# Expert loop of a routed MoE layer: index and gate copies moved between ScalarE, GpSimd and VectorE, and bounded gathers

## What is computed

```
scores = sigmoid(xt @ w_router)
_, top_idx = lax.top_k(scores + router_bias, 8)
gates = top_s / sum(top_s) * 2.5
xb = xt[tok_idx]
yb = (silu(xb @ w_gate[e]) * (xb @ w_up[e])) @ w_down[e]
routed = zeros.at[src_tok].add(yb * g[:, None])
```

## Time and profile before

| | us |
|---|---|
| median of 3 runs | 1636.74 |
| lowest, highest | 1635.55, 1638.66 |
| the profiled execution | 1641.21 |
| its span, first to last instruction | 1638.8 |
| busy: PE, DVE, ACT, POOL | 1498.1, 909.0, 562.4, 891.6 |
| mean granted clock of TensorE | 0.974 |

### The profile page before, as it was taken

One profiled execution on the slowest core, in us unless ns is written; L12 is line 12 of the kernel. 1 busy time (PEld: TensorE's weight loads), 2 busy tenths in 40 slices (PEclk: granted clock), 3 DMA queues, 4 the chain that ended last, 5 costly groups with the idle time before them and its releaser, 6 DMA issues.

```text
span 1638.8 us, 28709 instructions
## 1 busy us (share of the span) xinstructions
PE 1498.1 (91%) x9554; PEld 1276.1 (78%) x9554; DVE 909.0 (55%) x1595; ACT 562.4 (34%) x858; POOL 891.6 (54%) x1021
## 2 busy tenths in 40 slices
PE   6999999999799999889999999999999999999980
PEld 5789989989645666778888888888888888888870
DVE  4333788788678764455554454445454454444442
ACT  6434545444433322013333333333333333333333
POOL 0422235063203322467777777777777777777761
PEclk9999999999899999999999999999999999999995
DMA  5389321221250112379999999999999999999966
GB/s 182 98 290 309 120 78 51 77 67 49 103 200 27 41 51 99 121 261 315 327 302 335 308 313 308 315 319 320 315 323 316 316 310 312 325 307 305 321 184 220
DMA packets 104440, 366.18 MB, mean 223 GB/s; under 512 B 25976, under 2 KB 36121, under 8 KB 83407
## 3 DMA queue, kind: packets, MB, share of 16 engines
q1 hardware_dynamic: 60622, 246.60, 40.2%
q0 software_dynamic: 43776, 119.07, 26.8%
HBM read 300.68 MB, written 73.91 MB: 229 GB/s over the span
## 4 chain that ended last, share of the span: by engine, by line
POOL 25%; issue 18%; DMA 10%; POOLq 2%; PE 1%; DVE 1%; ACT 0%; DVEq 0%; ACTq 0%; SPq 0%
POOL wi L1636 16%; DMA acc_rows<-YE,sia 9%; POOL acc_rows L1660 4%; POOL acc_rows L1655 2%; POOL sia L1646 1%; POOL gta L1641 1%; DVE A L1875 1%; PE gu L1713 1%; DMA wi<-xn_rows,gi 1%; POOL sib L1647 0%; POOL gi L1628 0%; POOL gtb L1641 0%; POOLq L1628 0%; DMA A<-acc_rows 0%; POOLq L1687 0%
## 5 line engine op out<-in xcount | busy, mean ns | idle before, releaser
L1713 PE MATMUL gu<-XS,place 128*128 128x160 f32 x4160 | 577.8, 300 | 5.0 <-DVE XS L1829 5.0
L1713 PEld LDWEIGHTS gu<-XS,place 128*128 128x128 f32 x4160 | 573.9, 191 | 10.8 <-DVE XS L1829 5.8
L1636 POOL DMA_INDIRECT wi<-xn_rows,gi x320 | 408.1, 1275 | 132.5 <-issue 77.4
L1829 DVE STREAM_TRANSPOSE XS<-wi 128x1280 f32<-128x1280 f32 x65 | 163.3, 2512 | 369.9 <-DMA wi<-xn_rows,gi 343.4
L1773 ACT ACTIVATE SS<-gu 128x160 f32<-128x160 f32 x130 | 39.5, 304 | 399.0 <-PE gu L1713 399.0
L1123 POOL DMA_INDIRECT slot_table<-pay,si x64 | 62.2, 972 | 174.2 <-DVEq L1432 161.4
L1834 DVE TENSOR_TENSOR WL<-place,WH 128x2048 fp32r<-128x2048 f32 x65 | 146.7, 2258 | 14.1 <-ACT WH L1769 14.1
L1655 POOL DMA_INDIRECT acc_rows<-YF,sib x65 | 105.5, 1623 | 78.9 <-issue 33.5
L1783 ACT ACTIVATE YE<-ype,gta 128x512 f32<-128x512 f32 x130 | 89.4, 689 | 102.6 <-PE ype L1737 102.1
L1769 ACT ACTIVATE WH<-place 128x2048 fp32r<-128x2048 f32 x65 | 123.6, 1901 | 0.7 <-issue 0.7
L1724 PE MATMUL yrest<-place,HF 128*32 128x256 f32 x1040 | 72.5, 398 | 55.0 <-DVE WL L1834 54.9
(11 more groups left out here) (299 smaller groups left out, 2672.5 us busy)
## 6 DMA issues: line engine op xcount, KB each, us to landing
place<-in_w_gate_e SPq DMA_DIRECT2D x65, 1024.0 KB, 5.9
place<-in_w_up_e SPq DMA_DIRECT2D x65, 1024.0 KB, 8.9
place<-in_w_down_e SPq DMA_DIRECT2D x65, 1024.0 KB, 10.7
place<-in_w_in POOLq DMA_DIRECT2D x16, 512.0 KB, 7.2
late_parts<-wq_parts POOLq DMA_DIRECT2D x8, 1024.0 KB, 6.2
late_parts<-xn_parts POOLq DMA_DIRECT2D x8, 1024.0 KB, 5.7
wf_parts<-late_parts POOLq DMA_DIRECT2D x8, 1024.0 KB, 5.1
w_low<-late_parts POOLq DMA_DIRECT2D x8, 1024.0 KB, 5.2
```

What stands on the lines that cost most here:

```text
L1636: pool.indirect_dma_start(XQ[q][:, s * DQ:(s + 1) * DQ], None, quarters_d, bass.IndirectOffsetOnAxis(ap=index[s], axis=0)).then_inc(s_g[q] ...
L1713: last = pe.matmul(gu[f][:, k, :], raw[:, t, f * P:f * P + P], XS[:, q, t, :], start=(t == 0), stop=(t == KT - 1))
L1829: nc.vector.transpose(XS[:, q, :, :].rearrange("p t (s j) -> p s t j", s=RUNS), XQ[q].rearrange("p (s i t) -> p s t i", s=RUNS, t=KT)).the ...
```

## The change

In the expert loop:

- POOL copies nothing any more. The gate copies are gone: ScalarE's evictions read their scale from `K.gate` directly. The index copies `gi`, `sia`, `sib` are ScalarE activations (Copy): gi behind sigmoid(0), after a wait for the gather that last used it (s_g); sia and sib behind sigmoid(1), after a wait for the scatters of item n - 2 (s_ad). The semaphores s_gt and s_free go; what they held apart is now held by that wait.
- The gathers of the loop (items 1 to 65; item 0's is issued in the phase before) have a bound, 4 x 1024 - 1, and out of bounds is no error: rows of empty slots aren't fetched, and the buffer keeps what it held there. Their gate is 0 and their sums aren't scattered.
- VectorE's turn is low_down(n), hidden(0, n + 1), turned(n + 2), hidden(1, n + 1).
- The wait that POOL makes for the gather's landing before it reuses the buffer is now ScalarE's, by way of s_gi.

```diff
             def gather(q, n):
-                pool.tensor_copy(gi[q][:, :], K.quart[:, bass.ds(n * RUNS, RUNS)]).then_inc(s_gi, 1)
                 pool.wait_ge(s_gi, n - 1)
                 pool.sem_inc(turn["pool"], 1)
+                pool.wait_ge(s_xk, n - 1)
+                pool.sem_inc(turn["pool"], 1)
                 gather_runs(q, [gi[q][:, s:s + 1] for s in range(RUNS)])
...
-                                            bass.IndirectOffsetOnAxis(ap=index[s], axis=0)).then_inc(s_g[q], 16)
-
-            def gates(n, q):
-                for r in two:
-                    last = pool.tensor_copy(gt[q][r][:, :], K.gate[r][:, bass.ds(n, 1)])
-                last.then_inc(s_gt, 1)
+                                            bass.IndirectOffsetOnAxis(ap=index[s], axis=0),
+                                            bounds_check=QUARTERS * T - 1, oob_is_err=False).then_inc(s_g[q], 16)
...
             def add_rows(n, q):
-                pool.tensor_copy(si[q][0][:, :], K.idx[:, bass.ds(n, 1)]).then_inc(s_si, 1)
-                pool.tensor_copy(si[q][1][:, :], K.quart[:, bass.ds(n * RUNS + (RUNS - 1), 1)]).then_inc(s_si, 1)
                 if not isinstance(n, int) or n > 0:
                     pool.wait_ge(s_ad, n * 32)
-                    pool.sem_inc(s_free, 1)
-                pool.wait_ge(s_si, n * 2 + 2)
+                    pool.sem_inc(turn["pool"], 1)
+                pool.wait_ge(s_si, n + 1)
...
             def turn_(i, q, ahead):
                 n = i * 2 + q
-                if ahead >= 1:
-                    gates(n + 1, 1 - q)
                 if ahead >= 2:
-                    pool.wait_ge(s_g[q], i * LANDED + 2 * LANDED)
-                    pool.sem_inc(turn["pool"], 1)
-                    pool.wait_ge(s_xk, n + 3)
-                    pool.sem_inc(turn["pool"], 1)
                     gather(q, n + 4)
                 add_rows(n, q)
...
+            def gather_rows(q, n, landed):
+                act.wait_ge(s_g[q], landed)
+                act.sem_inc(turn["act"], 1)
+                act.activation(gi[q][:, :], K.quart[:, bass.ds(n * RUNS, RUNS)], ACT.Copy).then_inc(s_gi, 1)
+
+            def add_index(q, n, added):
+                if added is not None:
+                    act.wait_ge(s_ad, added)
+                    act.sem_inc(turn["act"], 1)
+                act.activation(si[q][0][:, :], K.idx[:, bass.ds(n, 1)], ACT.Copy)
+                act.activation(si[q][1][:, :], K.quart[:, bass.ds(n * RUNS + (RUNS - 1), 1)], ACT.Copy).then_inc(s_si, 1)
...
             def evict_rest(q, n):
-                act.wait_ge(s_gt, n + 1)
-                act.wait_ge(s_free, n + 1)
                 act.wait_ge(s_yr, n + 1)
-                act.activation(YF[q][:, :], yr[:, :], ACT.Copy, scale=gt[q][1][:, 0:1]).then_inc(s_yk, 1)
+                act.sem_inc(turn["act"], 1)
+                act.activation(YF[q][:, :], yr[:, :], ACT.Copy, scale=K.gate[1][:, bass.ds(n, 1)]).then_inc(s_yk, 1)
...
                 if ahead >= 1:
                     high_down(q, n, i + 1)
+                if ahead >= 1:
                     sigmoid(0, n + 1)
+                if ahead >= 3:
+                    gather_rows(q, n + 4, i * LANDED + 2 * LANDED)
                 if ahead == 1:
                     high_down(1 - q, n + 1, i + 2)
                 if ahead >= 1:
                     sigmoid(1, n + 1)
+                add_index(q, n, added)
                 evict_rest(q, n)
...
                 n, o = i * 2 + q, 1 - q
-                if ahead >= 2:
-                    turned(q, n + 2, i * LANDED + 2 * LANDED)
                 low_down(q, n)
                 if ahead >= 1:
                     hidden(0, o, n + 1)
+                if ahead >= 2:
+                    turned(q, n + 2, i * LANDED + 2 * LANDED)
+                if ahead >= 1:
                     hidden(1, o, n + 1)
```

More of the change, by code:

```diff
@@ L1546, in phase_experts @@
         si = [(sb(f"sia{i}", [P, 1], I32), sb(f"sib{i}", [P, 1], I32)) for i in two]
-        gt = [(sb(f"gta{i}", [P, 1]), sb(f"gtb{i}", [P, 1])) for i in two]
         quarters_d = xn2_d.rearrange("r (b n) -> (r b) n", b=QUARTERS)
@@ L1557, in phase_experts @@
         s_g = K.s_g
-        s_gt, s_ad, s_free = sem("gates_set"), sem("rows_added"), sem("rows_free")
+        s_ad = sem("rows_added")
         s_xk = sem("x_turned")
@@ L1570, in phase_experts @@
         outv = out.rearrange("b (j p) n -> p (b j) n", p=P)
-        turn = {e: sem(f"turn_{e}") for e in ("sp", "pool", "dve")}
+        turn = {e: sem(f"turn_{e}") for e in ("sp", "pool", "dve", "act")}
         block = ctx.enter_context(nc.Block())
@@ L1665, in turn_ @@
                 n = i * 2 + q
-                if ahead >= 1:
-                    gates(n + 1, 1 - q)
                 if ahead >= 2:
-                    pool.wait_ge(s_g[q], i * LANDED + 2 * LANDED)
-                    pool.sem_inc(turn["pool"], 1)
-                    pool.wait_ge(s_xk, n + 3)
-                    pool.sem_inc(turn["pool"], 1)
                     gather(q, n + 4)
                 add_rows(n, q)
-            pool.sem_inc(s_free, 2)
             gather_runs(1, [K.quart[:, RUNS + s:RUNS + s + 1] for s in range(RUNS)])
-            gates(0, 0)
             for q in two:
-                pool.wait_ge(s_g[q], LANDED)
-                pool.wait_ge(s_xk, q + 1)
                 gather(q, 2 + q)
@@ L1775, in evict_rest, with turn_ @@
             def evict_rest(q, n):
-                act.wait_ge(s_gt, n + 1)
-                act.wait_ge(s_free, n + 1)
                 act.wait_ge(s_yr, n + 1)
-                act.activation(YF[q][:, :], yr[:, :], ACT.Copy, scale=gt[q][1][:, 0:1]).then_inc(s_yk, 1)
+                act.sem_inc(turn["act"], 1)
+                act.activation(YF[q][:, :], yr[:, :], ACT.Copy, scale=K.gate[1][:, bass.ds(n, 1)]).then_inc(s_yk, 1)
             def evict(q, n, g):
                 act.wait_ge(s_y, n * 2 + (g + 4))
-                act.activation(YE[q][:, 512 * g:512 * g + 512], yp[g][:, :], ACT.Copy, scale=gt[q][0][:, 0:1]).then_inc(s_ya, 1)
-            def turn_(i, q, ahead):
+                act.sem_inc(turn["act"], 1)
+                act.activation(YE[q][:, 512 * g:512 * g + 512], yp[g][:, :], ACT.Copy, scale=K.gate[0][:, bass.ds(n, 1)]).then_inc(s_ya, 1)
+            def turn_(i, q, ahead, added):
                 n = i * 2 + q
@@ L1796, in turn_ @@
                     evict(q, n, g)
+            for q in two:
+                gather_rows(q, 2 + q, LANDED)
             sigmoid(0, 0)
@@ L1800, in _ @@
             last = pairs(act)
-            with act.Fori(0, last) as i:
+            for q in two:
+                turn_(0, q, 3, None)
+            with act.Fori(0, last - 1) as i:
                 for q in two:
[L1803 to L1806, removed]
+                    turn_(i + 1, q, 3, i * 64 + (q + 1) * 32)
+            turn_(last, 0, 2, last * 64)
+            turn_(last, 1, 1, last * 64 + 32)
+            turn_(last + 1, 0, 0, last * 64 + 64)
             act.activation(rt[:, 0:1], K.eps[:, 0:1], ACT.Sqrt).then_inc(s_r, 1)
```

## The result

| | us |
|---|---|
| before, median of 4 runs | 1637.58 (1635.55 to 1638.66) |
| after, median of 4 runs | 1583.43 (1582.39 to 1584.37) |
| after / before | 0.9671, 95% interval 0.9654 to 0.9687 |
| the profiled execution of after, its span | 1582.39, 1580.5 |

The account below looks back on a forecast made before the run. POOL's late gathers were taken to hold TensorE at 13.70 us a turn. Gains of 58.9 us (62 turns at 12.75) and 7.7 (end) took 1641.2 to 1574.6; adjusted to the median 1570, stated 1571, range 1562 to 1632.

Parts of the forecast that it names:

- A: Main case, expert loop: TensorE sets the pace, turns of 12.64 to 12.95 us, 1563 to 1585 us in all; chance 0.58.
- What bounds the kernel: Expert loop: POOL's late gathers delay transpose and WL, so TensorE loses 1.06 us a turn, 13.70 instead of 12.64.
- (1): POOL in the loop: five small copies leave, its two gaps fall to 0.30 us, saving 2.0 us a turn.
- (2): ScalarE in the loop: three more copies, 0.6 us a turn, covered by 4.04 us of standing; wait for s_g costs 0.
- (3): VectorE in the loop: WL before the transpose is ready 3.9 us ahead of yrest; the 52.1 us wait goes.
- (4): POOL's stall behind WL moves to the YF scatter, up to 2.0 us; POOL's turn 12.2 us, mean turn taken 12.75.
- (5): Loop gathers: the bound saves up to 0.48 us of DMA time and costs POOL 0.25 us a turn, 0.05 a gather.
- rival B: Expert loop: DMA takes over as the limit, between 1585 and 1632 us in all; chance 0.20.
- (6): After the last gate/up: with POOL on time only items 62 to 64 remain to add; gain 7.7 us.
- The start: First gate/up to that of item 2: forecast difference 0 us.

Follow-up runs that it names:

- copies_only: The changed kernel with VectorE's old order and without the bound on the gathers, so only the copies have moved; 1587.5 us, 0.9739 of before.
- order_only: The kernel before with VectorE's new order alone (transpose behind hidden(0)), copies still on POOL, no bound; 1640.0 us, 1.0027 of before.
- dummy_copies: The changed kernel with five copies of the old sizes back on POOL, writing a tile nothing reads, a wait behind each group; 1703.5 us, 1.0387 of before.
- old_order: The changed kernel with VectorE's old order, bound and moved copies kept; 1593.8 us, 0.9725 of before.
- tail_wait: The changed kernel, but in its last three turns ScalarE waits for the scatters of item n - 2, not n - 1; 1587.3 us, 0.9677 of before.
- spaced_more: The changed kernel; POOL begins gathers of items 2 to 5 only after the first half of gate/up of items 0 to 3 respectively; 1574.4 us, 0.9619 of before.
- bound_only: The kernel before with the bound on the loop's gathers alone; 1647.8 us, 1.0082 of before.

## Why the prediction was right

The main case, A, is what happened: TensorE sets the pace, and the measured 1583.43 lies in A's own range, 1563 to 1585, at its end. By the steps:

- *What bounds the kernel*: right. copies_only, order_only and dummy_copies show that POOL's issue was the bound. That SP's loads had time to spare was also right: in the changed kernel they still stand 369.9 us for TensorE between 740 and 1500 us, at a DMA share of 1.00.
- *(1) The copies, 2.0 us of POOL a turn*: the mechanism is right. Their price in another setting isn't fixed: put back in dummy_copies they made turns of 14.48 us against 12.65.
- *(2) ScalarE*: the copies take 0.20 us each as forecast. The wait for the gather is 21.4 us in all and harmless. But I priced the wait for s_ad only as a replacement of s_free; it stands 142 us in all. It costs nothing in the loop because its cover, the slack of WH and WL ahead of yrest, is larger, but it eats into that cover: behind the wait of 2.58 us that ends at 898.19 WL is ready at 906.11, 1.7 us before yrest, and behind the one of 3.07 us that ends at 911.32 it is ready 3.1 us before, where the prediction had 3.9.
- *(3) VectorE's order*: the wait for WL is gone, but the order isn't what removes it: in copies_only, with the old order, it is 0.6 us between 760 and 1500 us, and 3.8 in old_order. As an explanation, this step gave the order too much: on-time gathers alone do it. The order is worth 0.12 us a turn with the bound and 0.03 without it.
- *(4) The stall behind WL*: it exists as forecast, but at a gather (the first or second in 48 of 59 turns between 760 and 1500 us) and not at YF. The step took POOL to add item n in turn n; it stays an item behind (see the end), so gathers and not the YF scatter meet WL. The sum there also left out the bound's own 0.25 us a turn, which would have made POOL's 12.2 us 12.45. The mean turn, 12.65, is better than the 12.75 that I kept for it; this is the term that was mis-sized by 0.1 x 62 = 6 us.
- *(5) The bound*: 0.05 us a gather, as forecast. The copy that starts 1.01 us into the scatter spoke for a small price, but the figure itself was a choice. So at most a small part of the scatters' 0.6 us more can be the bound's; what the rest is no run shows. The DMA rival B didn't come: with and without the bound TensorE nearly keeps its pace (12.65 and 12.68), at a DMA share of 1.00 either way.
- *(6) The end*: wrong, by 9.7 us. It took POOL to be on time and adds for items 62 to 64 alone to remain. In fact POOL's add of item 61 begins at 1519.28, after the last gate/up's start, one item behind as before. The scatters' own loop, landing plus 2.9 us, is as long as TensorE's turn, so POOL doesn't catch up; the landing of 9.5 to 11.7 us that the chain shows within the loop never entered the sum. That this loop is the reason is read from the trace, as no run shortened a landing. The wait for one item too many in the last turns was also missed, but tail_wait shows that this is not where the time is.
- *The start*: missed. It was costed at nothing, without a look at what else the copies did there: they broke a row of fifteen gathers. spaced_more gives the time back: its start is 23.6 us, 7.9 less, and its median saves 61.8 us on the 1636.2 of before beside it, where the change saves 54.2.

The two misses (7.7 and 9.7) and the better loop (-6.1), with -3.1 of scatter ahead of the loop, make +8.3 of span; the rest of the 12.4 us between 1571 and 1583.43 is in the main that the profiled execution of before lay 4.5 us above its median. That the time still lies in A's own range, 1.6 us from its end, is in part luck: 17.4 us of misses were partly made up by a better loop than the sum had.

## What to carry to other kernels

When one engine's issue is gapless and its consumers all wait a little, take work off that engine first; a new order downstream and fewer bytes are worth next to nothing until then, as order_only and bound_only show. Then sum every loop that closes over a DMA's landing as if it were an engine: here scatter, landing and next scatter is as long as the matmuls' turn, and the kernel ends with four of them in a row. And an instruction that is removed may have been a useful pause: compare the first turns of both traces, not only the steady ones.

## What the runs showed of the hardware

- GpSimd's work is held up by the VectorE tensor_tensor that makes WL from two SBUF operands (128x2048, 2.3 us), whatever GpSimd is at: a gather of 1.00 us became 2.34, a scatter of 1.58 became 3.19 (tail_wait), two copies that together take 0.3 us became 2.34 (dummy_copies). The gather and the scatter ended 1.0 and 1.4 us after it. Moving either only changed which one was hit.
- A bound on an indirect DMA's index costs 0.05 us a DMA (0.989 to 1.040 us), and fewer bytes are moved, as the rows out of bounds are left out (1.17 to 1.04 MB a turn).
- On the chain of the changed kernel an accumulating scatter of 128 rows of 4 KB lands 9.5 to 11.7 us after its start beside a DMA share of 1.00, and 4.6 to 6.3 us after it at the end, where the share is 0.07 to 0.62.
- TensorE can stand in gaps for which the profile shows no semaphore, in a stretch that it passes for the first time, while GpSimd issues ten or more DMAs in an unbroken row: with the fall of the granted clock that follows (1.00 to 0.75 and 0.81) it costs 7 to 8 us in after, and nothing in spaced_more, which breaks the rows. order_only has breaks and still three short gaps. The cause isn't settled.
